# Loading the conv rows of a hybrid decoder layer late, reordering its opening stage, and adding identity transposes on TensorE

## The reference

```python
shift1, scale1, gate1, shift2, scale2, gate2 = split(c @ w_ada + b_ada, 6)   # c: 9 condition rows
h  = rms_norm(x, g_pre_mix) * (1 + scale1) + shift1
z  = h @ w_in                 # mLSTM q,k,v,o and i/f gates; attention q,k,v; two merge gates
...                           # mLSTM scan, differential attention, merge, w_out
x  = x + gate1 * rms_norm(y, g_post_mix)
h2 = rms_norm(x, g_pre_ffn) * (1 + scale2) + shift2
a, b = split(h2 @ w_up, 2)
conv = conv_b + sum_j conv_w[j] * concat([conv_state, a])[j:j+T]   # width 3, D_FF = 2816 channels
x  = x + gate2 * rms_norm((gelu(conv) * b) @ w_down, g_post_ffn)
```

## Time and profile before

| | |
|---|---|
| median of 3 runs | 1798.46 us (1796.12 to 1800.38) |
| the profiled execution | 1796.01 us, of which the traced span is 1794.3 us |
| TensorE (PE) busy | 1745.5 us, 97% of the span |
| VectorE, ScalarE, GpSimd busy | 752.3, 500.9, 154.5 us (42%, 28%, 9%) |
| granted TensorE clock, mean | 0.994 of 2.4 GHz |
| DMA | 190.26 MB in all; 9, 6 and 6 tenths busy in the first three fortieths of the span |

### The profile page before, as it was taken

How to read it: one execution, slowest core, us unless ns; L and a number is a source line. 1 busy time by engine, 2 the same in 40 slices (tenths; PEclk the granted TensorE clock), 3 DMA queues, 4 the chain that set the end, 5 groups by cost and what they waited for, 6 DMA issues and landing times. The chain is left out here.

```text
span 1794.3 us, 27250 instructions
## 1 busy us (share of the span) xinstructions
PE 1745.5 (97%) x11470; PEld 1654.8 (92%) x11470; DVE 752.3 (42%) x1017; ACT 500.9 (28%) x810; POOL 154.5 (9%) x231
## 2 busy tenths in 40 slices
PE   5999999999999999999999999999999999999998
PEld 5899988888888899999988899999999999999997
DVE  5522144544440146465534344424534434344345
ACT  4311134444333335431233331111211211211212
POOL 4010000000010014400022300000000000000001
PEclk8999999999999999999999999999999999999999
DMA  9665242242228576343532211111111021011004
GB/s 319 233 202 182 100 147 84 92 128 71 91 77 256 165 231 169 102 121 121 189 123 72 77 48 47 48 47 48 47 47 47 24 71 48 24 59 55 28 29 170
DMA packets 159697, 190.26 MB, mean 106 GB/s; under 512 B 13693, under 2 KB 138125, under 8 KB 159564
## 3 DMA queue, kind: packets, MB, share of 16 engines
q1 hardware_dynamic: 139368, 170.95, 29.7%
q10 hardware_dynamic: 19208, 17.43, 3.0%
q0 software_dynamic: 1008, 0.23, 0.1%
HBM read 146.70 MB, written 41.87 MB: 105 GB/s over the span
## 5 line engine op out<-in xcount | busy, mean ns | idle before, releaser
L158 PE MATMUL ps<-mg_hi,w_hi 128*128 128x352 f32 x1008 | 218.1, 324 | 2.0 <-ACT a_ext L2721 2.0
L158 PE MATMUL ps<-mg_hi,w_lo 128*128 128x352 f32 x1008 | 217.3, 323 | 0.0
L158 PE MATMUL ps<-mg_lo,w_hi 128*128 128x352 f32 x1008 | 217.0, 323 | 0.0
L158 PEld LDWEIGHTS ps<-mg_hi,w_hi 128*128 128x128 f32 x1008 | 171.6, 189 | 2.5 <-issue 1.9
L158 PEld LDWEIGHTS ps<-mg_hi,w_lo 128*128 128x128 f32 x1008 | 173.1, 188 | 0.0
L158 PEld LDWEIGHTS ps<-mg_lo,w_hi 128*128 128x128 f32 x1008 | 171.2, 188 | 0.0
L2814 DVE TENSOR_TENSOR f_t<-f_t,ps 128x1056 f32<-128x1056 f32 x80 | 100.3, 1254 | 151.2 <-PE ps L158 151.2
L143 DVE TENSOR_TENSOR w_lo<-w_raw,w_hi 128x2048 fp32r<-128x2048 f32 x61 | 141.3, 2316 | 50.2 <-ACT w_hi L139 50.1
L139 ACT ACTIVATE w_hi<-w_raw 128x2048 fp32r<-128x2048 f32 x61 | 116.7, 1913 | 121.0 <-PE ps L158 120.0
L1224 PE MATMUL ps<-acts_hi,w_hi 128*128 128x352 f32 x384 | 132.8, 346 | 6.6 <-ACT out_z L1074 3.8
L1340 PE MATMUL ps<-acts_hi,w_hi 128*128 128x352 f32 x384 | 128.0, 333 | 4.7 <-PEq L993 1.6
(11 more groups left out here) (412 smaller groups left out, 3066.0 us busy)
## 6 DMA issues: line engine op xcount, KB each, us to landing
w_raw<-in_w_in SPq DMA_DIRECT2D x22, 1024.0 KB, 5.7
w_raw<-in_w_up SPq DMA_DIRECT2D x22, 1024.0 KB, 5.1
w_ada_chunks<-in_w_ada ACTq DMA_DIRECT2D x16, 1024.0 KB, 7.3
w_raw<-in_w_down SPq DMA_DIRECT2D x11, 1024.0 KB, 4.9
z_scratch<-out_z SPq DMA_DIRECT2D x48, 176.0 KB, 1.8
z_scratch<-gate_ev SPq DMA_DIRECT2D x48, 176.0 KB, 4.4
w_ada_chunks<-in_w_ada SPq DMA_DIRECT2D x8, 1024.0 KB, 10.5
chunks<-z_scratch SPq DMA_DIRECT2D x24, 256.0 KB, 4.1
```

The source lines that it names most:

```text
L158: mm = pe.matmul(ps[:, bank + b, 0:TB], w[wi][:, k, j * P:(j + 1) * P], (a_hi, a_lo)[ai][:, k, b * TB:(b + 1) * TB], start=(n == 0), stop= ...
```

## The change

Four things are done, all in the first block.

- The conv rows are no longer loaded at the start. SP loads them as 40 half rows of 1408 into `conv_rows`, in a slot of `w_ada_chunks`, once all pairs are done, ahead of the last weight load of this block. TensorE transposes them in 11 pieces ahead of the last tile, and VectorE copies them to `ff_t`. The `if_raw` load moves behind w_ada chunk 7 and the weights of chunk 1, and what is made from it behind the four quarters.
- Condition pair 0 and its columns are moved ahead of the last x tiles on TensorE, ScalarE and VectorE.
- `w_hi` and `w_lo` of chunk 0 are made in two pieces, the first quarter (channel blocks 0 and 1) apart, and the products of block 0 run in the order high x high, high x low (w_lo), low x high, each behind its own wait.
- TensorE transposes the identity matrix into a PSUM bank that nobody reads: 16 times before x tile 0, twice before tiles 1, 3 and 4.

```diff
@@ SP
                 load_ada(sp, 3)
-                sp.dma_start(if_raw[:], ...).then_inc(s_if, 16)
                 for n in range(WS, FIRST):
                     sp.wait_ge(s_ada, (n - WS) // 2 + 1)
                     load_ada(sp, n)
                 load_chunk(sp, 1, w_cols(I["w_in"][0], D_COL + NC_), KT)
+                sp.dma_start(if_raw[:], ...).then_inc(s_if, 16)
...
+                sp.wait_ge(s_ada, PAIRS)
+                for r, rows_of in ((0, I["state_conv"][0].rearrange("b w (h f) -> (b w h) f", h=2)),
+                                   (32, I["conv_w"][0].rearrange("w (h f) -> (w h) f", h=2)),
+                                   (38, I["conv_b"].rearrange("a (h f) -> (a h) f", h=2))):
+                    sp.dma_start(conv_rows[r:r + rows_of.shape[0], :], rows_of).then_inc(s_ffl, 16)
                 c = IN_CHUNKS - 1
                 load_chunk(sp, c % 2, w_cols(I["w_in"][0], NC_), KT, c + 1)
@@ ACT
-                act.dma_start(ffrows[0:16, :], I["state_conv"][0].rearrange("b w f -> (b w) f")).then_inc(s_ffl, 16)
-                act.dma_start(ffrows[16:19, :], I["conv_w"][0]).then_inc(s_ffl, 16)
-                act.dma_start(ffrows[19:20, :], I["conv_b"]).then_inc(s_ffl, 16)
...
+                x_square(1)
+                for t in range(NTT):
+                    if t + 2 < NTT:
+                        x_square(t + 2)
+                    x_cols(t)
+                    if t == 4:
+                        condition(0)
-                split_hi(act, 0, 16)
+                act.wait_ge(w_loaded[0], 16)
+                act.activation(w_hi[:, 0, W_FIRST], w_raw[:, 0, W_FIRST], ACT.Copy).then_inc(w_hi_first, 1)
                 for q in range(4):
-                    if q:
+                    if q > 1:
                         condition(q)
                     for i in range(2):
                         act.wait_ge(s_hm, 4 * q + 3 + i)
                         act.activation(acts_hi[:, 2 * q + i, :], x_t[:, 2 * q + i, :], ACT.Copy).then_inc(s_ahi, 1)
+                        if (q, i) == (0, 0):
+                            condition(1)
+                    if q == 0:
+                        act.activation(w_hi[:, 0, W_REST], w_raw[:, 0, W_REST], ACT.Copy).then_inc(w_hi_ready, 1)
@@ DVE
+                    if t == 8:
+                        dve.wait_ge(s_vect, 5)
+                        condition_cols(0)
...
-                    if q == 0:
-                        split_lo(dve, 0, 1)
+                    for part, hi_done, lo_done in ([(W_FIRST, w_hi_first, w_lo_first)], [(W_REST, w_hi_ready, w_lo_ready)], [], [])[q]:
+                        dve.wait_ge(hi_done, 1)
+                        dve.tensor_tensor(w_lo[:, 0, part], w_raw[:, 0, part], w_hi[:, 0, part].bitcast(F32), ALU.subtract).then_inc(lo_done, 1)
                     low(2 * q)
                     low(2 * q + 1)
...
+                    if c == IN_CHUNKS - 1:
+                        dve.wait_ge(s_conv_tr, 1)
+                        dve.tensor_copy(ff_t[:].rearrange("p (h k) r -> p h k r", h=2),
+                                        ps[:, BA, 0:20 * FT].rearrange("p (k r h) -> p h k r", k=FT // 2, h=2)).then_inc(s_conv, 1)
                     out_tile(c)
@@ PE
+                def keep_busy(n):
+
+                    for _ in range(n):
+                        pe.transpose(ps[:, BT, 0:P], ident[:], ident[:])
+
+                keep_busy(16)
                 x_tr(0)
+                keep_busy(2)
                 x_tr(1)
...
+                            pe.wait_ge(s_ffl, 48)
+                            pe.wait_ge(s_arow, PAIRS)
+                            for k in range(FT // 2):
+                                tr = pe.transpose(ps[:, BA, 40 * k:40 * (k + 1)], conv_rows[:, k * P:(k + 1) * P], ident[0:40, 0:40])
+                            tr.then_inc(s_conv_tr, 1)
                             last_tile(c)
```

More of the change, by code:

```diff
@@ L842, in slot, with first_products @@
                         condition_tr(pair_in(s - 1))
+                def first_products(k, n, j):
+                    w = [x[:, 0, :].rearrange("p (k n) -> p k n", k=KT) for x in (w_hi, w_lo)]
+                    wi, ai = ((0, 0), (0, 1), (1, 0))[n]
+                    for b in range(NTB):
+                        mm = pe.matmul(ps[:, 3 * j + b, 0:TB], w[wi][:, k, j * P:(j + 1) * P],
+                                       (acts_hi, acts_lo)[ai][:, k, b * TB:(b + 1) * TB],
+                                       start=(k == 0 and n == 0), stop=(k == KT - 1 and n == 2))
+                    return mm
                 def first_tiles(k):
                     pe.wait_ge(s_alo, k + 1)
-                    w = [x[:, 0, :].rearrange("p (k n) -> p k n", k=KT) for x in (w_hi, w_lo)]
                     for j in range(2):
-                        for n, (wi, ai) in enumerate(((0, 0), (0, 1), (1, 0))):
-                            for b in range(NTB):
-                                mm = pe.matmul(ps[:, 3 * j + b, 0:TB], w[wi][:, k, j * P:(j + 1) * P],
-                                               (acts_hi, acts_lo)[ai][:, k, b * TB:(b + 1) * TB],
-                                               start=(k == 0 and n == 0), stop=(k == KT - 1 and n == 2))
+                        for n in range(3):
+                            mm = first_products(k, n, j)
                         if k == KT - 1:
                             mm.then_inc(tile_done, 1)
+                def keep_busy(n):
+                    for _ in range(n):
+                        pe.transpose(ps[:, BT, 0:P], ident[:], ident[:])
+                keep_busy(16)
                 x_tr(0)
+                keep_busy(2)
                 x_tr(1)
@@ L862, in _ @@
                 x_tr(2)
-                pe.wait_ge(s_ffl, 48)
-                for k in range(FT):
-                    tr = pe.transpose(ps[:, BT, 20 * k:20 * (k + 1)], ffrows[:, k * P:(k + 1) * P], ident[0:20, 0:20])
-                tr.then_inc(s_vecp, 1)
-                for t in range(3, 8):
-                    x_tr(t)
-                pe.wait_ge(s_vect, 6)
+                keep_busy(2)
+                x_tr(3)
+                keep_busy(2)
+                x_tr(4)
+                pe.wait_ge(s_vect, 5)
                 pe.wait_ge(s_sel, 3)
                 condition(0)
+                x_tr(5)
+                x_tr(6)
+                condition_tr(0)
+                x_tr(7)
                 x_tr(8)
-                condition_tr(0)
                 for half in range(2):
@@ L876, in _ @@
                 condition(1)
-                pe.wait_ge(w_lo_ready, 1)
-                first_tiles(0)
+                pe.wait_ge(w_hi_first, 1)
+                pe.wait_ge(s_ahi, 1)
+                for j in range(2):
+                    first_products(0, 0, j)
                 condition_tr(1)
+                pe.wait_ge(w_lo_first, 1)
+                for j in range(2):
+                    first_products(0, 2, j)
+                pe.wait_ge(s_alo, 1)
+                for j in range(2):
+                    first_products(0, 1, j)
                 first_tiles(1)
                 condition(2)
+                pe.wait_ge(w_lo_ready, 1)
                 first_tiles(2)
```

78 lines of the change are left out of this document (36 added, 42 removed).

## The result

The changed kernel takes 1789.52 us (median of 5 runs, 1789.11 to 1789.76) against 1799.75 (5 runs, 1796.12 to 1800.99). The medians lie 10.2 us apart. The ratio is one of means: 0.9946, interval 0.9933 to 0.9959, or 9.7 us less. The prediction said 1791.1, between 1787.5 and 1796.0. The profiled execution took 1789.57 us with a span of 1787.8. That is 6.5 less than the span of before, whose execution (1796.01) lies just under the lowest of its kernel's five runs.

A forecast was written before the change was run, and what follows sets the result against it. TensorE, busy 97%, was taken as the bound, with the moment of its first input projection product. Start -6.2, clock -2.1, conv transposes +0.9 gave -7.4 us: 1788.6 profiled, 1791.1 as median, range 1787.5 to 1796.0.

The follow-up runs named there:

- the further order: Changed kernel without its 22 identity transposes, condition pair 0 behind x tile 5, second half of pair 1 behind the first six products: 1788.53 us, ratio 0.9945.
- the second trace of the changed kernel: Trace from the second series of the changed kernel, run again unchanged on another chip: 1788.78 us, ratio 0.9947 to before.

## What to carry to other kernels

- Small tables that land as long rows on a few partitions should not be queued ahead of loads that something waits for; here the same bytes in short pieces over all partitions cost no time that could be told. Look for a dip of the rate at a high DMA share (170 GB/s at 0.91).
- A filler for the clock is worth something only where the faster instructions behind it are the last to arrive. Here the next thing was a load, so 22 of them bought nothing.
- When one engine's order is changed to reach its bound sooner, check which waits are left in front of the first dense stretch: in the further order a start won by 3.2 us at 1.2 GHz gave its lead back.
- Compare waits over several traces of each kernel before calling a difference chance: the clock's falls moved from trace to trace, the wait for w_lo did not.

## What the runs showed of the hardware

- Transposes raise the clock. In the second trace of the changed kernel TensorE had done eight small transposes of c_rows and then only identity transposes; the x transposes from 8.63 took 1.09 us, not 1.97:

```profile
4.04 3.46 PE L881 MATMUL ps<-ident 128*128 128x128 f32 x16
8.63 1.09 PE L815 MATMUL ps<-ident,x_in 128*128 128x128 f32 x8 [1.13 <-DVE x_in L614]
```

  The Trainium skill, "TensorE: Matmul & The Clock Gate", section "Part 4: PE-mode transpose", says that they don't count; here the measurement decides against it, for transposes of float32 as this kernel makes them.
- In the changed kernel the x transposes ran at the high clock from 8.63 on in the second trace and only from about 12.6 on in the first, with the fillers at 4.04 and 4.17; and the clock fell at 20.8, at 26.3 or not. A single trace doesn't tell what fillers do.
- 220 KB as 20 rows on 20 partitions delayed a load queued far behind them by 2.5 us more than the same bytes in short pieces on 128 partitions.
